# Three low parts a layer on GpSimd, two fewer tap pairs on TensorE, and another order in the first mixer and the cross heads

## The chip, the cores and the metric

One core of a Trainium2 chip runs the whole program: two decoder blocks on a sequence of 256 rows. The metric is the device time of one execution in microseconds. TensorE (PE), VectorE (DVE), ScalarE (ACT), GpSimd (POOL) and SyncE (SP) have instruction streams of their own, are written one by one in the kernel, and meet only at semaphores.

## What is computed

The reference is two networks one after the other. The first has two layers (a mixer, cross attention to a memory, a feed-forward with squared ReLU), the second two more. Cut to what matters here:

```python
# first block, layer 0: window attention and a gated linear recurrence, then memory_xattn, then the MLP
q, k, v, xr, gate = split(rms_norm(x) @ w_in)
o_a = dilated_window_attn(q, k, v)              # four heads ("at0")
xc = conv4(xr); a, u = gates(xc)
hs = associative_scan(a, u)                     # the scan
x = x + concat([o_a, hs * gelu(gate)]) @ w_out
x = x + memory_xattn(rms_norm(x), mem)          # four heads of 256 ("xa0", "xa1")
x = x + square(relu(rms_norm(x) @ w1)) @ w2

# second block, two layers
x = x + 0.5 * swiglu(rms_norm(x))
u = rms_norm(x) @ w_in
y = a * sigmoid(gate)                           # 384 channels
y = depthwise_conv(y, w_dw, taps=31) + b_dw     # causal, one filter a channel
y = silu(layer_norm(y))
o = sliding_window_attention(q, k, v, sinks)    # six heads ("sw", pairs 0 to 2), block 128
m = memory_attention(mq, mk, mv)                # four heads (pairs 3 and 4)
x = x + concat([y, o, m]) @ w_out
x = x + 0.5 * swiglu(rms_norm(x)); x = rms_norm(x)
```

## The kernel before

**Weights in units.** All weights pass as 269 units of 128 x 2048 (1 MB), in the order of use. For each unit SyncE issues a transfer into `raw`, ScalarE rounds it into `w_hi` (`highs`, L1024), and VectorE forms the low part, the rest `raw - w_hi`, in place of `raw` (`lows`, L1582). TensorE multiplies by high and low parts, so that two passes give nearly the precision of f32 (L360 to L362, L369 to L372, L405 to L407). There are 6 places for `raw` and the low parts and 4 for the high parts: a transfer waits until the unit six before it is used up, a high half until the unit four before. `highs(n)` and `lows(n)` work off all units up to n, and from unit 20 on one more (`prepared`). Unit numbers of a layer of the second block count from `u0`; `L_WO` = 42 is the first of the four units of its output projection, so `L_WO + 1` to `+ 3` are 43, 44 and 45.

**The order of the work** is written out by hand for each engine. An instruction that waits holds up all behind it on its engine. `mark` gives an instruction a semaphore count and `at` is what another waits for.

**First mixer.** TensorE sums the squares of the rows (`stream_sums`), VectorE turns the sums into a mean (`mean`, L1614), GpSimd takes the root (L2258), VectorE builds a diagonal matrix of it (`diagonal`, L1631), and TensorE spreads it over the columns (`spread`, L485). Between them VectorE also forms the low halves of the memory (`memory_low`, L1653). Later come the four heads: scores (L509), largest value and exponentials, `normalized` rows on VectorE (L1727, L1731), `turned` on TensorE (L519), copied by ScalarE, `product` (L529). The scan (L1914) and its gate (L1918) lie between them on VectorE. `key_columns` (L490) turns the normalized keys of the cross attention; tile t goes to its own PSUM bank, and bank 0 holds a value product before, which ScalarE copies out (`vxcopy`).

**Cross heads** (`cross`). For each of four heads TensorE makes the query, ScalarE squares it (L1317), VectorE adds and scales it (`query`, L1939, L1941), `soft` handles the maximum and ScalarE the exponentials, VectorE normalizes, TensorE turns and multiplies.

**Window stage of the second block.** The depthwise convolution has 384 channels, three blocks of 128. The third block is done on TensorE alone (`third_channel`, L895: products of 128 x 128 with diagonal-like tiles, 16 shifts times 2 groups, two taps each). Of the first two blocks VectorE does the first 24 taps (`run_taps`, one instruction of 128 x 256 a tap and block, L2109) and TensorE the last 7, as 4 shifts x 2 groups x 2 blocks. `third_channel(n)` issues the next n of these products, first those of the two shared blocks into bank 4; ScalarE copies their sums out (`second`, L1517) before the third block may use the bank. In between run the five pairs of heads: `window_scores` (L846, L852), VectorE's row maxima (`soft`: TENSOR_REDUCE L2147 and, for the window heads, a minimum with the sinks, L2153), ScalarE's exponentials (L1475), `window_turned` (L861), ScalarE's `turned_copy` (L1483), `window_product` (L874), `normalized_rows` (L2176), `rows_turned` (L921). GpSimd takes the roots of the head norms before this stage (L2258) and that of the channel variance (`cms`) behind it.

```python
def soft(i):
    nm = b.by_head(W_NM, range(2 * i, 2 * i + 2))                                  # in stat, SBUF
    for t in range(NT):
        m = dve.tensor_reduce(nm[:, t, :], W.scores(b, i, t), AX.X, ALU.max, negate=True)   # from PSUM
    if i < 3:
        sink = b.stat[:, W_NSINK + 2 * i:W_NSINK + 2 * i + 2].unsqueeze(1).broadcast_to([P, NT, 2])
        m = dve.tensor_tensor(nm, nm, sink, ALU.min)                               # both in SBUF
```

## Time and profile before

| | us |
|---|---|
| median of 3 runs (1679.78 to 1681.53) | 1679.93 |
| the profiled execution | 1680.01 |
| its span, first to last instruction | 1678.7 |
| TensorE matmuls busy | 1661.4 (99%) |
| VectorE busy | 1194.3 (71%) |
| ScalarE busy | 881.9 (53%) |
| GpSimd busy | 175.3 (10%) |

Busy shares say which engine is close to its limit, not how much a shorter instruction gives: matmuls overlap, so their busy time also covers gaps of up to 0.2 us. What an edit is worth is read from the starts of TensorE's instructions and from what it waits for. One matmul of f32 operands stands as two records in the trace.

### The profile page before, as it was taken

How to read it: one execution, taken by the hardware profiler on the slowest of the kernel's cores; microseconds unless marked ns; L12 is line 12 of the kernel's file. 1: busy time of each engine (PE TensorE's matmuls, PEld its weight loads, DVE VectorE, ACT ScalarE, POOL GpSimd, SP SyncE). 2: the span in 40 equal slices, each digit the busy share in tenths (PEclk: the TensorE clock that was granted, in tenths of full speed). 3: DMA queues.
4: the chain of work that ended last, by engine and by line, in shares of the span. 5: the costliest groups of instructions: out<-in, count | busy, mean ns of one | idle time of the engine just before them, and what ended most of it. 6: DMA issues, size and time to landing. Idle time of an engine off the chain costs nothing.

```text
span 1678.7 us, 24718 instructions
## 1 busy us (share of the span) xinstructions
PE 1661.4 (99%) x10347; PEld 1480.4 (88%) x10348; DVE 1194.3 (71%) x1450; ACT 881.9 (53%) x1094; POOL 175.3 (10%) x166
## 2 busy tenths in 40 slices
PE   8999999999999999999999999999999999999998
PEld 7889988888999888888889998888888899998887
DVE  7876477665656777577767877778687677787763
ACT  6655455444545455455544564556555545565552
POOL 0401010011101001200021110003200022010002
PEclk9999999999999999999999999999999999999999
DMA  8444345555434565555555335555554654145541
GB/s 338 170 150 158 115 167 195 183 194 204 161 112 163 189 214 188 193 191 178 202 222 197 117 110 191 179 197 203 184 195 182 236 203 176 51 176 188 188 181 46
DMA packets 42991, 297.39 MB, mean 177 GB/s; under 512 B 4864, under 2 KB 5632, under 8 KB 8448
## 3 DMA queue, kind: packets, MB, share of 16 engines
q1 hardware_dynamic: 39600, 282.61, 46.7%
q10 hardware_dynamic: 3280, 13.21, 2.1%
q8 instruction: 81, 1.33, 0.3%
q14 instruction: 30, 0.25, 0.1%
HBM read 294.75 MB, written 1.05 MB: 176 GB/s over the span
## 4 chain that ended last, share of the span: by engine, by line
PE 93%; DVE 4%; ACT 2%; DMA 1%; issue 1%; SPq 0%; POOL 0%; ACTq 0%; DVEq 0%
PE ps L372 38%; PE ps L371 19%; PE ps L360 4%; PE ps L362 4%; PE ps L361 4%; PE ps L369 4%; PE ps L405 3%; PE ps L407 3%; PE ps L406 3%; PE ps L370 2%; DVE w_lo L1582 1%; ACT w_hi L1024 1%; PE ps L895 1%; PE ps L529 1%; PE ps L874 1%
## 5 line engine op out<-in xcount | busy, mean ns | idle before, releaser
L1582 DVE TENSOR_TENSOR w_lo<-raw,w_hi 128x2048 fp32r<-128x2048 f32 x267 | 610.4, 2289 | 210.4 <-ACT w_hi L1024 206.6
L1024 ACT ACTIVATE w_hi<-raw 128x2048 fp32r<-128x2048 f32 x267 | 508.3, 1905 | 184.6 <-PE ps L372 117.8
L372 PE MATMUL ps<-xT,w_hi 128*128 128x512 f32 x1680 | 598.6, 396 | 0.0
L371 PE MATMUL ps<-xT,w_lo 128*128 128x256 f32 x1680 | 468.7, 279 | 0.0
L372 PE MATMUL ps<-hT,w_hi 128*128 128x512 f32 x1147 | 405.2, 397 | 0.0
L372 PEld LDWEIGHTS ps<-xT,w_hi 128*128 128x128 f32 x1680 | 315.3, 188 | 65.0
L371 PEld LDWEIGHTS ps<-xT,w_lo 128*128 128x128 f32 x1680 | 316.7, 189 | 11.2 <-DVE xT L1589 0.2
L371 PE MATMUL ps<-hT,w_lo 128*128 128x256 f32 x1147 | 321.4, 280 | 1.4 <-DVE hT L1781 1.4
L372 PEld LDWEIGHTS ps<-hT,w_hi 128*128 128x128 f32 x1147 | 215.4, 188 | 50.1
L371 PEld LDWEIGHTS ps<-hT,w_lo 128*128 128x128 f32 x1147 | 216.3, 189 | 4.7 <-DVE hT L1781 2.7
L1076 ACT ACTIVATE tmp<-ps 128x512 f32<-128x512 f32 x120 | 72.0, 600 | 254.5 <-PE ps L372 254.5
L2291 POOL TENSOR_TENSOR ff<-ff 128x256 f32<-128x256 f32 x70 | 94.1, 1344 | 962.7 <-ACT ff L1054 669.1
L360 PE MATMUL ps<-xT,w_hi 128*128 128x256 f32 x608 | 176.5, 290 | 1.8 <-DVE w_lo L1816 1.8
L362 PE MATMUL ps<-xT,w_hi 128*128 128x256 f32 x608 | 171.9, 283 | 0.0
L361 PE MATMUL ps<-xT,w_lo 128*128 128x256 f32 x608 | 171.9, 283 | 0.0
L1640 DVE TENSOR_TENSOR tmp<-ps,tmp 128x512 f32<-128x512 f32 x120 | 82.7, 689 | 83.6 <-ACT tmp L1076 83.4
L360 PEld LDWEIGHTS ps<-xT,w_hi 128*128 128x128 f32 x608 | 116.5, 192 | 3.2 <-DVE w_lo L1816 2.5
L361 PEld LDWEIGHTS ps<-xT,w_lo 128*128 128x128 f32 x608 | 116.5, 192 | 0.5
L362 PEld LDWEIGHTS ps<-xT,w_hi 128*128 128x128 f32 x608 | 116.4, 192 | 0.0
L369 PE MATMUL ps<-xT,w_hi 128*128 128x512 f32 x240 | 96.4, 403 | 0.0
L405 PE MATMUL ps<-w_hi,memT 128*128 128x256 f32 (+1 forms) x256 | 81.0, 317 | 0.0
L2258 POOL TENSOR_TENSOR stat<-stat,mhalf 128x2 f32<-128x2 f32 (+2 forms) x45 | 42.1, 944 | 365.1 <-DVE stat L1678 112.7
(282 smaller groups left out, 2003.6 us busy)
## 6 DMA issues: line engine op xcount, KB each, us to landing
raw<-weights_dram SPq DMA_DIRECT2D x263, 1024.0 KB, 4.8
tmp<-third_taps_dram ACTq DMA_DIRECT2D x2, 2048.0 KB, 9.2
raw<-weights_dram SPq DMA_DIRECT2D x4, 768.0 KB, 5.1
raw<-weights_dram SPq DMA_DIRECT2D x4, 512.0 KB, 8.5
tmp<-mem_dram ACTq DMA_DIRECT2D x2, 1024.0 KB, 7.0
x<-x_in_dram SPq DMA_DIRECT2D x2, 512.0 KB, 5.6
arena<-mem_dram ACTq DMA_DIRECT2D x1, 1024.0 KB, 10.4
arena<-pool_mat_dram ACTq DMA_DIRECT2D x1, 1024.0 KB, 6.9
```

Of the source, the lines that this page charges most:

```text
L360: pe.matmul(out, b.hi(u, cs), src[:, k, 0, :], start=first, stop=False)
L361: pe.matmul(out, b.lo(u, cs), src[:, k, 0, :], start=False, stop=False)
L362: return pe.matmul(out, b.hi(u, cs), src[:, k, 1, :], start=False, stop=last)
L369: pe.matmul(ps[:, bank, :].rearrange("p (a n) -> p a n", a=2), hi, src[:, k, :, :], start=True, stop=False)
L371: pe.matmul(ps[:, bank, 0:S], lo, src[:, k, 0, :], start=False, stop=False)
L372: return pe.matmul(ps[:, bank, :].rearrange("p (a n) -> p a n", a=2), hi, src[:, k, :, :], start=False, stop=last)
L405: pe.matmul(out, h, b.hi(u, cs), start=(first and j == 0), stop=False)
L1024: act.activation(b.hi(u, slice(0, width(u))), b.raw(u, slice(0, width(u))), ACT.Copy).then_inc(*mark("hi", u))
L1076: act.activation(tmp, ps[:, bank:bank + 2, S:2 * S], ACT.Copy).then_inc(*mark("half", name, j))
L1582: dve.tensor_tensor(b.lo(u, cs), b.raw(u, cs), b.hi(u, cs).bitcast(F32), ALU.subtract).then_inc(*mark("lo", u))
L1640: dve.tensor_tensor(dst, ps[:, bank:bank + 2, 0:S], tmp, ALU.add).then_inc(*mark(label, *((name, j) if label != "u32" else (name[:-1], j))))
L2291: pool.tensor_tensor(b.acc(), b.sq(0) if c == 1 else b.acc(), b.sq(c), ALU.add).then_inc(*mark("sqsum", f, c))
```

## The change

Four things change. The low parts of units 43, 44 and 45 of each layer of the second block are formed by GpSimd, after its roots of the head norms, and no longer by VectorE; TensorE waits for them by a semaphore of their own (`low_of`). `SHARED` goes from 4 to 2: VectorE does the first 28 taps of the first two blocks, TensorE the last 3, and the table of their tiles (`shared_taps`) is half as wide and lies in one place. The numbers of taps and products between the steps of the window stage are set anew, on ScalarE the memory values are copied before the first turned rows and the memory keys after the second sums. In the first mixer and the cross heads instructions stand in another order.

```diff
+GPSIMD_UNITS = frozenset(U_LAYER + PER_LAYER * l + L_WO + i for l in range(2) for i in (1, 2, 3))
+def low_of(u):
+    return ("lo_gpsimd" if u in GPSIMD_UNITS else "lo"), u
-SHIFTS, SHARED = 16, 4
+SHIFTS, SHARED = 16, 2
...
@@ TensorE, first mixer @@
-    pe.wait_ge(*at("vxcopy", 0, 2))
-    key_columns(0, 0, (0, 1))
+    key_columns(0, 0, (0, 1), (1, 0), lambda: pe.wait_ge(*at("vxcopy", 0, 2)))
...
@@ TensorE, window stage @@
         window_turned(0)
-        third_channel(4)
         window_turned(1)
...
         window_scores(2)
-        third_channel(4)
+        third_channel(6)
         window_product(1)
...
         memory_columns("mq", qr[:, :, 512:768])
-        third_channel(6)
+        third_channel(5)
...
@@ ScalarE, window stage @@
         soft(0)
         soft(1)
-        turned_copy(0)
...
         c.then_inc(*mark("mvcopy", l))
+        turned_copy(0)
         turned_copy(1)
-        memory_keys()
         act.wait_ge(*at("second_sum", l))
...
         i.then_inc(*mark("second", l))
+        memory_keys()
...
@@ ScalarE, behind the first feed-forward of a layer @@
-        for dst, cs in ((b.arena[:, 5, :], slice(0, 1024)), (b.arena[:, 15, 512:1024], slice(1024, 1536))):
-            act.dma_start(dst, d["shared_taps"][l, :, cs]).then_inc(*landed("d_shared", l, cs.start))
-        act.dma_start(b.slot2(0)[:, :, 768:1024],
-                      d["shared_taps"][l, :, 1536:2048].rearrange("p (a n) -> p a n", a=2)).then_inc(*landed("d_shared", l))
+        act.dma_start(b.arena[:, 5, :], d["shared_taps"][l]).then_inc(*landed("d_shared", l))
...
@@ VectorE, lows() @@
+            if u in GPSIMD_UNITS:
+                continue
...
@@ VectorE, first mixer @@
+    mean("x0", 4)
+    diagonal("x0")
     for c in range(4):
         memory_low("mem1", raw1, c)
-    mean("x0", 4)
     lows(4)
-    diagonal("x0")
...
     lows(16)
+    lows(17)
+    normalized("at0", 3, True)
+    head_low("at0", 1, slice(4, 6), 2)
     dve.wait_ge(*at("scan_in"))
...
-    lows(17)
-    head_low("at0", 1, slice(4, 6), 2)
-    normalized("at0", 3, True)
...
@@ VectorE, cross heads @@
         lows(uq + 4)
+        normalized(tag, 0)
         query(2)
-        normalized(tag, 0)
         soft(1)
+        normalized(tag, 1)
         lows(uq + 5)
         query(3)
-        normalized(tag, 1)
...
@@ VectorE, window stage @@
-        lows(u0 + L_MQ + 4)
-        run_taps(12)
+        run_taps(15)
         soft(2)
         run_taps(9)
         soft(3)
         sink_arguments()
-        lows(u0 + L_MK + 3)
-        run_taps(5)
+        run_taps(7)
         soft(4)
         normalized_rows(SWA)
+        run_taps(5)
+        row_lows(SWA)
         run_taps(4)
-        lows(u0 + L_MV + 3)
-        run_taps(3)
-        row_lows(SWA)
-        run_taps(2)
         normalized_rows(MEM)
...
@@ GpSimd, after the roots of the head norms @@
+        first = U_LAYER + PER_LAYER * l + L_WO + 1
+        for u in range(first, first + 3):
+            cs = slice(0, width(u))
+            pool.wait_ge(*at("hi", u))
+            pool.tensor_tensor(b.lo(u, cs), b.raw(u, cs), b.hi(u, cs).bitcast(F32),
+                               ALU.subtract).then_inc(*mark("lo_gpsimd", u))
```

Line numbers in what follows of the change are those of the changed file, which are up to 7 higher (L1582 is L1587 there, L2109 is L2114).

VectorE at the start of the window stage, before: row maxima of the first two pairs (L2147, L2153), a low part, taps (L2109).

```order
L1684 TENSOR_TENSOR arena<-ps,stat 128x256 x2
L2147 TENSOR_REDUCE stat<-ps 128x2 x2
L2153 TENSOR_TENSOR stat<-stat 128x2x2
L2147 TENSOR_REDUCE stat<-ps 128x2 x2
L2153 TENSOR_TENSOR stat<-stat 128x2x2
L1582 TENSOR_TENSOR w_lo<-raw,w_hi 128x2048
L2109 SCALAR_TENSOR_TENSOR arena<-arena,par 128x256 x12
L2147 TENSOR_REDUCE stat<-ps 128x2 x2
L2153 TENSOR_TENSOR stat<-stat 128x2x2
L2109 SCALAR_TENSOR_TENSOR arena<-arena,par 128x256 x9
```

And of the change:

```order
L1689 TENSOR_TENSOR arena<-ps,stat 128x256 x2
L2152 TENSOR_REDUCE stat<-ps 128x2 x2
L2158 TENSOR_TENSOR stat<-stat 128x2x2
L2152 TENSOR_REDUCE stat<-ps 128x2 x2
L2158 TENSOR_TENSOR stat<-stat 128x2x2
L2114 SCALAR_TENSOR_TENSOR arena<-arena,par 128x256 x15
L2152 TENSOR_REDUCE stat<-ps 128x2 x2
L2158 TENSOR_TENSOR stat<-stat 128x2x2
L2114 SCALAR_TENSOR_TENSOR arena<-arena,par 128x256 x9
```

The low part between the second minimum and the first taps is gone, and 15 taps follow instead of 12.

GpSimd at the same place, of the change: the roots of the head norms, then the three low parts, then the root of the channel variance and the sums of squares. Before, the row of L2380 is not there.

```order
L2371 MEMSET arena 128x8
L2259 TENSOR_TENSOR stat<-stat,mhalf 128x8 x2
L2259 TENSOR_TENSOR stat<-stat,mhalf 128x4 x4
L2380 TENSOR_TENSOR w_lo<-raw,w_hi 128x2048 x3
L2259 TENSOR_TENSOR stat<-stat,mhalf 128x2
L2292 TENSOR_TENSOR ff<-ff 128x256 x6
```

They stand behind the four roots of four columns (two each for the memory queries and keys of the window stage), and nothing but their high halves holds them.

VectorE in the first mixer before, from the normalized rows of the third head (L1731): low part, scan (L1914), gate (L1918), low part, low half of the first heads (L1737), then the last head's rows (L1720 to L1731).

```order
L1731 TENSOR_SCALAR arena<-arena,stat 128x256
L1582 TENSOR_TENSOR w_lo<-raw,w_hi 128x2048
L1914 SCALAR_TENSOR_TENSOR arena<-arena 128x256 x4
L1918 SCALAR_TENSOR_TENSOR arena<-arena 128x1024
L1582 TENSOR_TENSOR w_lo<-raw,w_hi 128x2048
L1737 TENSOR_TENSOR xT<-ps,xT 128x2x256
L1720 SCALAR_TENSOR_TENSOR arena,stat<-arena,tmp 128x128
L1720 SCALAR_TENSOR_TENSOR arena,stat<-arena,tmp 128x256
L1727 RECIPROCAL stat<-stat 128x2
L1731 TENSOR_SCALAR arena<-arena,stat 128x128
L1731 TENSOR_SCALAR arena<-arena,stat 128x256
```

And of the change:

```order
L1736 TENSOR_SCALAR arena<-arena,stat 128x256
L1587 TENSOR_TENSOR w_lo<-raw,w_hi 128x2048 x2
L1725 SCALAR_TENSOR_TENSOR arena,stat<-arena,tmp 128x128
L1725 SCALAR_TENSOR_TENSOR arena,stat<-arena,tmp 128x256
L1732 RECIPROCAL stat<-stat 128x2
L1736 TENSOR_SCALAR arena<-arena,stat 128x128
L1736 TENSOR_SCALAR arena<-arena,stat 128x256
L1742 TENSOR_TENSOR xT<-ps,xT 128x2x256
L1922 SCALAR_TENSOR_TENSOR arena<-arena 128x256 x4
L1926 SCALAR_TENSOR_TENSOR arena<-arena 128x1024
```

Both low parts and the last head's rows now stand before the scan.

## Rows read from the trace of the kernel before

**Rows 1.** The page, parts 1 and 2: TensorE's busy time, and its granted clock.

```profile
PE 1661.4 (99%) x10347; PEld 1480.4 (88%) x10348; DVE 1194.3 (71%) x1450; ACT 881.9 (53%) x1094; POOL 175.3 (10%) x166
PEclk9999999999999999999999999999999999999999
```

**Rows 2.** TensorE's waits: us in total, times, longest.

```profile
PE ps L519 <- DVE arena L1731: 3.3, 5, 1.4
PE ps L485 <- DVE ff L1631: 2.4, 2, 1.9
...
PE ps L490 <- ACT tmp L1137: 0.3, 1, 0.3
```

**Rows 3.** Timeline near the first spread: start, us, engine, line, operation, [idle].

```profile
25.68 0.16 DVE L1614 TENSOR_SCALAR stat<-ps 128x2 f32<-128x2 f32 x1
27.08 2.29 DVE L1582 TENSOR_TENSOR w_lo<-raw,w_hi 128x2048 fp32r<-128x2048 f32 x1 [1.18 <-ACT w_hi L1024]
...
29.83 0.70 PE L485 MATMUL ps<-ff,cst 128*128 128x256 f32 x2 [1.89 <-DVE ff L1631]
```

**Rows 4.** Timeline of TensorE: product and transposes, without and with a wait.

```profile
107.48 0.81 PE L529 MATMUL ps<-arena 128*128 128x256 f32 x4
108.13 0.49 PE L519 MATMUL ps<-cst,arena 128*128 128x128 f32 x3
...
113.95 0.81 PE L529 MATMUL ps<-arena 128*128 128x256 f32 x4
116.13 0.55 PE L519 MATMUL ps<-cst,arena 128*128 128x128 f32 x3 [1.37 <-DVE arena L1731]
```

**Rows 5.** Timeline of TensorE: the first of four such waits in the cross heads.

```profile
171.35 0.66 PE L519 MATMUL ps<-cst,arena 128*128 128x128 f32 x4 [0.48 <-DVE arena L1731]
```

**Rows 6.** Timeline of TensorE: eight calls of the grouped products.

```profile
944.04 1.95 PE L895 MATMUL ps<-pairs,arena 128*128 128x128 f32 x16
945.83 0.60 PE L911 MATMUL ps<-cst,arena 128*128 128x128 f32 x4
```

**Rows 7.** GpSimd beside VectorE: one line's min/median/max in ns, then timelines.

```profile
L2291 POOL TENSOR_TENSOR ff<-ff x70: 733/891/2542, 146.3 to 1663.1; 128x256 f32<-128x256 f32 x70
...
48.92 2.54 POOL L2323 TENSOR_TENSOR arena<-arena 128x1024 f32<-128x1024 f32 x1
49.23 2.50 DVE L1853 SCALAR_TENSOR_TENSOR arena<-arena,sm 128x256 f32<-128x256 f32 x1
...
74.83 2.41 POOL L2339 TENSOR_TENSOR arena<-arena 128x1024 f32<-128x1024 f32 x1 [6.62 <-ACT arena L1243]
...
1178.12 3.02 POOL L2304 TENSOR_TENSOR ff<-ff 128x256 f32<-128x256 f32 x2 [7.89 <-ACT ff L1048]
1180.60 0.41 DVE L1795 TENSOR_TENSOR ff<-ps,ff 128x256 f32<-128x256 f32 x1
```

**Rows 8.** Timelines of the window stage of the first layer, by engine.

```profile
939.40 1.98 POOL L2258 TENSOR_TENSOR stat<-stat,mhalf 128x4 f32<-128x4 f32 x2 [1.13 <-DVE stat L1678]
...
944.08 0.16 DVE L2153 TENSOR_TENSOR stat<-stat 128x4 f32<-128x4 f32 x1
...
946.36 4.83 DVE L2109 SCALAR_TENSOR_TENSOR arena<-arena,par 128x256 f32<-128x256 f32 x12
...
936.55 1.96 ACT L1024 ACTIVATE w_hi<-raw 128x2048 fp32r<-128x2048 f32 x1
...
943.08 2.60 ACT L1475 ACTIVATE arena<-ps,stat 128x128 f32<-128x128 f32 x8 [3.26 <-DVE stat L2153]
947.12 0.81 ACT L1483 ACTIVATE arena<-ps 128x768 f32<-128x768 f32 x1 [1.44 <-PE ps L861]
947.83 0.83 ACT L1508 ACTIVATE arena<-ps,stat 128x256 f32<-128x256 f32 x2
...
947.82 0.82 PE L861 MATMUL ps<-cst,arena 128*128 128x128 f32 x6
948.76 0.41 PE L874 MATMUL ps<-arena 128*128 128x65 f32 x2
```

More of the change, by code:

```diff
@@ L177, in taps_of @@
         j = 2 * SHARED * block + 2 * (s - SHIFTS + SHARED) + g
-        place, at = ((5, P * j) if j < 8 else (15, 512 + P * (j - 8)) if j < 12 else ((j - 12) // 2, 768 + P * (j % 2)))
-        return self.arena[:, place, at:at + P]
+        return self.arena[:, 5, P * j:P * j + P]
     def by_head(self, col, heads):
@@ L374, in up_unit @@
     def up_unit(u, bank, of=None):
-        pe.wait_ge(*at("lo", u))
+        pe.wait_ge(*at(*low_of(u)))
         if of is None:
@@ L388, in head_unit @@
     def head_unit(u, bank, of=None):
-        pe.wait_ge(*at("lo", u))
+        pe.wait_ge(*at(*low_of(u)))
         out = b.pair(bank)
@@ L415, in rows_units @@
                 between(k)
-            pe.wait_ge(*at("lo", u))
+            pe.wait_ge(*at(*low_of(u)))
             for t in range(NT):
@@ L424, in value_unit @@
     def value_unit(u, bank):
-        pe.wait_ge(*at("lo", u))
+        pe.wait_ge(*at(*low_of(u)))
         for t in range(NT):
@@ L435, in out_projection @@
             u = u0 + i
-            pe.wait_ge(*at("lo", u))
+            pe.wait_ge(*at(*low_of(u)))
             if i < 3:
@@ L491, in chunk_transposes, with key_columns @@
         return last
-    def key_columns(l, pair, banks):
+    def key_columns(l, pair, banks, order=(0, 1), between=None):
         tag = f"xk{l}{pair}"
-        for t in range(NT):
+        for t in order:
             pe.wait_ge(*at("hrow", tag, t))
+            if between and t == order[1]:
+                between()
             chunk_transposes(banks[t], b.k_rows(pair)[:, t, :], 4).then_inc(*mark("ctr", tag, t))
@@ L563, in feed_forward @@
                 if at_tile % 16 == 0:
-                    pe.wait_ge(*at("lo", v))
+                    pe.wait_ge(*at(*low_of(v)))
                 if oc == 0 and kc % 2 == 0:
@@ L659, in tensor_program @@
     u = U_KEYS[0][1]
-    pe.wait_ge(*at("lo", u))
+    pe.wait_ge(*at(*low_of(u)))
     for t in range(NT):
@@ L665, in tensor_program @@
     turned("at0", 2, 0)
-    pe.wait_ge(*at("lo", u + 1))
+    pe.wait_ge(*at(*low_of(u + 1)))
     for t in range(NT):
@@ L681, in second_keys @@
         if (k, bk) == (5, 0):
-            pe.wait_ge(*at("kcol", "xk00", 1))
+            pe.wait_ge(*at("kcol", "xk00", 0))
             key_columns(0, 1, (0, 1))
@@ L752, in tensor_program @@
     feed_forward("mlp0", U_FF[0], False, sums_in_6("mlp0"), spread_in_6("mlp0"))
-    pe.wait_ge(*at("lo", U_POOL))
+    pe.wait_ge(*at(*low_of(U_POOL)))
     for g in range(4):
@@ L828, in memory_tile @@
                 last.then_inc(*mark("unit", u))
-        pe.wait_ge(*at("lo", u0 + L_MK))
+        pe.wait_ge(*at(*low_of(u0 + L_MK)))
         pe.wait_ge(*at("hrow", f"qk{l}", 0))
@@ L836, in tensor_program @@
             chunk_transposes(1 + t, qr[:, t, 0:512], 4).then_inc(*mark("ctr", f"qk{l}", t))
-        pe.wait_ge(*at("lo", u0 + L_MV))
+        pe.wait_ge(*at(*low_of(u0 + L_MV)))
         pe.wait_ge(*at("hrow", f"qk{l}", 1))
@@ L940, in tensor_program @@
         window_turned(2)
-        third_channel(6)
+        third_channel(5)
         window_product(2)
@@ L945, in tensor_program @@
         window_turned(3)
-        third_channel(5)
+        third_channel(4)
         rows_turned(SWA)
@@ L1125, in head_high, with key_copies @@
                        ACT.Copy).then_inc(*mark("ohi", tag, i))
-    def key_copies(tag, dst8, banks, pair):
-        for t in range(NT):
+    def key_copies(tag, dst8, banks, pair, order=(0, 1)):
+        for t in order:
             act.wait_ge(*at("ctr", tag, t))
@@ L1300, in scalar_program @@
     head_high("at0", 3, slice(6, 8), 3, U_V + 1)
-    key_copies("xk00", b.k8(), (0, 1), 0)
+    key_copies("xk00", b.k8(), (0, 1), 0, (1, 0))
     key_copies("xk01", b.k8(), (0, 1), 1)
```

## The prediction

> **What bounds the kernel now.** I read the page's busy times first: TensorE is busy 99% of the span, at its upper clock of 2.4 GHz in every slice [rows 1]. Busy matmuls overlap, so I then read TensorE's waits: all that the profile names are some 12 us, and three of them lie where this change works [rows 2]. So TensorE's own stream of instructions sets the time. An edit is worth what it takes out of that stream, or out of a stall in it, and work moved between the other engines costs nothing until something that TensorE waits for comes late. The places themselves are read in the timeline, from start to start. The profiled execution took 1680.0 us, of which its span is 1678.7 and 1.3 lie around it; the median of the three runs is 1679.9, so I work from 1680.0.
>
> **First mixer, the spread of x0.** TensorE waits 1.89 for VectorE's diagonal [rows 3]. VectorE reads the column sums at 25.68, behind four memory lows, and then works on a low part from 27.08 to 29.3 before it builds the diagonal [rows 3]. In the new order the mean and the diagonal stand before both. The low part ahead of them ends near 23.2; with 0.3 for the two small operations, 0.7 for GpSimd's root and 0.5 for the diagonal it is there at about 25, before TensorE is at the spread (27.9). The low part behind it begins at 27.08 because it waits for its high half [rows 3], so it isn't late. The wait is gone.
>
> **The heads.** TensorE waits 3.3 us in five places for normalized softmax rows: once 1.37 in the first mixer [rows 4], four times 0.48 in the two cross attentions (one is shown [rows 5]), and 0.28 for a value copy before the first key columns [rows 2]. In the mixer the rows stand behind scan, gate and a low part on VectorE; in the new order VectorE, which ends the low part before that at 108.3, does one more until 110.5 and has the rows at 112.0, before TensorE starts the third product at 113.95. The scan's result comes 4.4 later (a low part, the softmax rows, a head's low half), near 116.3; the low half made from it is wanted by the second unit of the output projection, near 129. In the cross heads the exponentials are done some 4 us before the query for which VectorE now no longer waits first. The key columns in the order 1, 0 put 0.43 of transposes ahead of the wait for the copy. All six waits go: 1.9 + 3.3 + 0.3 = 5.5. With each wait a restart goes too: 113.95 to 116.13 is 2.18, the same pair without a wait 0.65 (107.48 to 108.13) [rows 4], so 1.53 are lost where the wait is 1.37. I take 0.16 for each of six: 1.0. **Gain 6.5.**
>
> **The convolution.** The grouped products were 48 calls a layer (16 of the first two blocks, 32 of the third) and are 40. A call is two records; 16 records take from 944.04 to 945.83 [rows 6], so a call is 0.224 and 8 are **1.8 a layer**, all in TensorE's stream. VectorE gets 8 more taps of 0.40 (12 in 4.83 [rows 8]), 3.2, and gives away three low parts of 2.3: by its own time it is better off by 3.7. The shared taps come in one transfer instead of three, long before they are read: nothing.
>
> **The low parts on GpSimd.** This decides. An addition of 256 columns takes GpSimd 0.73 at best, one of 1024 columns 2.41 [rows 7]: 2.19 ns a column, so 4.65 for 2048. And it does not run beside VectorE: a VectorE step on two SBUF operands, which takes 0.40 a piece in a row of them [rows 8], took 2.50 when it began 0.3 behind a GpSimd operation of 2.54, that is, it ended with it [rows 7]. An operation with one operand in PSUM passes: 0.41 at 1180.60, while GpSimd is at work until 1181.14 [rows 7]. The Trainium skill, GPSIMD Engine Reference, section Performance versus the Vector engine, has 4.5 us for an addition of 2048 columns; by it each low part would hold VectorE 0.15 less and the sum below would be 0.9 lower.
>
> So I lay out the window stage anew, in the first layer (the second has the same rows 482 us later). GpSimd is free at 941.4 (939.40 + 1.98) and the high halves of units 43 and 44 are written (the second at 938.5) [rows 8]: low parts from 941.4 to 946.0 and on to 950.7. VectorE's row maxima read PSUM and pass, but each pair ends in a minimum of 4 columns on two SBUF operands. The first minimum, due at 942.9, gets in at 946.0 between the two low parts; the second, 944.08 before [rows 8], is held until 950.7. ScalarE's exponentials of that pair (1.3, half of 2.60 [rows 8]) end at 952.1, and TensorE, which turned the pair at 947.82, does so at 952.2. Behind the exponentials ScalarE has a value copy of 0.83 and a copy of turned rows of 0.81, so the first product starts at 953.9 instead of 948.76 [rows 8]: **5.1 late**. Of the 8 calls that are gone, 4 lay before it and are swallowed; 4 lie behind it and give 0.9 back.
>
> VectorE from there: 15 taps end at 956.8, the third maximum 958.0, 9 taps 961.6, the fourth 962.9, 7 taps 965.8, the fifth, whose scores are late too, 967.5, the rows of the window heads 968.9, where TensorE asks at 968.7. Then the third low part, whose high half is written behind the fourth pair's exponentials, starts at 967.5 and holds the next 5 taps until 972.1; the rows of the memory heads come at 977.7, where TensorE asks at 976.8. These two waits are 1.1, of which I count 0.5, since waits of 0.1 to 0.3 that the stretch has anyway (the first product waited 0.29 behind the transposes: 0.94 instead of 0.65 [rows 8]) vanish in them. **Loss 5.1 - 0.9 + 0.5 = 4.7 a layer**; the 1.8 saved is inside it. Queued behind the low parts on GpSimd is only the root of the channel variance, wanted 12 us after the last of them, and TensorE reads units 43 to 45 later still.
>
> **Sum:** 1680.0 - 6.5 + 2 x 4.65 = **1682.8**. What a measurement can tell from no change is 0.2%, 3.4 us: 1676.6 to 1683.3.
>
> **Bounds of what the trace doesn't show.** Whether an operation of 4 columns is held: from below nothing, from above the rest of the low part. I take the upper end, since the rows that are held and those that pass differ by their operands. The Trainium skill, SBUF — State Buffer, section Who interferes with whom, has the rule without a width in it: two SBUF inputs are enough to be locked out for the whole GpSimd instruction. By the rule the sum is 1682.8; if only wide operations are held it is rival (a). Whether 2048 columns hold as 1024 do: from below nothing (c), from above longer (b).
>
> **Rivals.**
> (a) Only the taps are held. Then the first product starts at 948.0, but the taps begin at 950.7 instead of 946.36, of which 15 end near 956.4; third maximum, exponentials and transposes follow late, and TensorE's line turns into waits one after the other. I get 3.3 a layer: 1680.0 - 6.5 + 6.7 = **1680.2**. For it: nothing so narrow was seen held.
> (b) The other side: a low part is longer beside VectorE than its width says. The median of 256 columns is 0.89 against 0.73 [rows 7]; by that ratio, 1.22, a low part is 5.7. Two stand before the second minimum and the third before the memory rows, so each us on a low part is 3 a layer: 1682.8 + 6 x 1.0 = **1689**. It decides from 4.75 on. Against it: the 1024 columns at 48.92, with VectorE held, took 2.54, only 0.13 more than alone. TensorE also stands still for 4 us here; the granted clock never leaves its upper level in this trace [rows 1], and the longest gap in TensorE's starts is 2.2 [rows 4]. The Trainium skill, TensorE: Matmul & The Clock Gate, Part 1, lets an idle TensorE fall to half its clock; no row here shows it, and it would add to this case.
> (c) No hold at this width. Then each layer saves its 1.8 and the small waits before the first product, 2.3: 1680.0 - 6.5 - 4.6 = **1668.9**. Against it: the 2.50.
> (d) The hold is real, but the stage has more slack than I find, and its loss and the 1.8 cancel: **1673.5**, the first block's gain alone.
>
> **How the numbers follow.** Forecast 0.34, (a) 0.22, (b) 0.18, (c) 0.14, (d) 0.12. The forecast lies 0.5 under the edge of what counts as slower: 0.22 within, 0.12 slower; (a) 0.18 within, 0.03 faster, 0.01 slower. Faster 0.29, within 0.40, slower 0.31. The range reaches to (c) below, which the rows don't exclude, and nearly to (b) above: 1668 to 1688. The forecast's own is 1680 to 1685.
>
> **What would show it.** In the first 500 us the waits of 1.9, 1.4, 0.3 and four of 0.5 gone from TensorE's list. GpSimd's low parts at 4.6 us. In the window stage a minimum of 3 to 4 us instead of 0.16, a tap of 4, and a TensorE wait of about 4 for ScalarE's exponentials of the second pair. I am wrong if the minimum stays at 0.16 and the first product isn't late, if the taps aren't held, or if the first block's waits come back at another tile.

## The result, and the profile after

| | before | changed |
|---|---|---|
| median of 6 runs each, us | 1680.0 | 1686.8 |
| lowest to highest | 1679.8 to 1681.8 | 1685.4 to 1689.0 |
| the profiled execution, and its span | 1680.0, 1678.7 | 1686.9, 1685.5 |

The ratio is 1.0039, 95% interval 1.0027 to 1.0051: slower by 0.4%. The forecast was 1682.8, with a range of 1668 to 1688, of which 1680 to 1685 was the forecast's own and the rest was there for its rivals. Each ratio further down is to runs of the kernel before that were taken beside it, with medians of 1679.9 to 1680.6; one run of e2, 2731.9 us at a mean clock of 0.555, is left out as slow.

The page of the changed kernel, in the lines of [rows 1]; each digit of the second is the granted clock in tenths, in a fortieth of the span. (All lines of code stand 5 to 7 further down: L868 was L861, L902 was L895, L2158 was L2153.)

```profile
PE 1664.7 (99%) x10316; PEld 1485.0 (88%) x10316; DVE 1205.0 (71%) x1460; ACT 881.3 (52%) x1094; POOL 202.3 (12%) x172
PEclk9999999999999999999999899999999999899999
```

The clock line now has two digits of 8. They are the slices in which the two window stages lie. TensorE's waits, with the total, the number of times and the longest, as in [rows 2]:

```profile
PE ps L868 <- ACT arena L1478: 9.1, 4, 3.6
...
PE ps L491 <- DVE ff L1636: 0.5, 1, 0.5
...
PE ps L928 <- DVE arena L2181: 0.3, 2, 0.2
```

Of [rows 2], the 3.3 for the softmax rows and the 0.3 for the value copy are gone, and of the two waits for a diagonal only the one of 0.5 at the end of the program is left. In their place stands one group: the transposes of the window stage (L868) wait 9.1 for ScalarE's exponentials, in each layer once 0.96 for the first pair and once 3.59 for the second. Next the window stage of the first layer, by engine. POOL's two rows are the low parts, DVE's are the row maxima (L2152), the minima (L2158) and taps (L2114), and the last four are TensorE's:

```profile
934.48 9.04 POOL L2380 TENSOR_TENSOR w_lo<-raw,w_hi 128x2048 fp32r<-128x2048 f32 x2
964.09 4.54 POOL L2380 TENSOR_TENSOR w_lo<-raw,w_hi 128x2048 fp32r<-128x2048 f32 x1 [20.58 <-ACT w_hi L1030]
...
936.00 3.07 DVE L2158 TENSOR_TENSOR stat<-stat 128x4 f32<-128x4 f32 x1
939.00 1.01 DVE L2152 TENSOR_REDUCE stat<-ps 128x2 f32<-128x256 f32 x2
940.11 3.43 DVE L2158 TENSOR_TENSOR stat<-stat 128x4 f32<-128x4 f32 x1
943.46 6.01 DVE L2114 SCALAR_TENSOR_TENSOR arena<-arena,par 128x256 f32<-128x256 f32 x15
...
965.98 4.51 DVE L2114 SCALAR_TENSOR_TENSOR arena<-arena,par 128x256 f32<-128x256 f32 x5
...
937.17 1.95 PE L902 MATMUL ps<-pairs,arena 128*128 128x128 f32 x16
...
944.98 1.54 PE L868 MATMUL ps<-cst,arena 128*128 128x128 f32 x6 [3.59 <-ACT arena L1478]
946.50 2.79 PE L881 MATMUL ps<-arena 128*128 128x65 f32 x12
...
977.35 1.46 PE L963 MATMUL ps<-arena,cst 128*128 128x256 f32 x6
```

Two low parts take 9.04, so 4.52 each. The minimum of 4 columns, 0.16 before [rows 8], takes 3.07 and 3.43. Each ends with a low part: 936.00 + 3.07 = 939.07 and 934.48 + 4.52 = 939.00, then 943.54 and 943.52. The second minimum is what ScalarE's exponentials wait for, and TensorE stands still for 3.59. The reductions between them, which read PSUM, take 1.01 for two as ever. The third low part holds taps: five of them take 4.51 from 965.98, where five took 2.06 before.

The third view is the same stage cut into stretches, with the granted clock behind the busy times:

```profile
934.00:945.00 11.00, 6.45 (x55) 5.78 (x51) 10.25 (x11) 2.78 (x9) 9.52 (x3) 0.96 0.27 95
945.00:955.00 10.00, 10.00 (x50) 8.63 (x51) 7.81 (x21) 4.48 (x10) 0.00 (x0) 0.54 0.00 0
955.00:965.00 10.00, 10.00 (x85) 9.06 (x85) 7.14 (x18) 6.25 (x13) 0.91 (x1) 1.00 0.01 2
```

Behind the wait the clock is 0.54 for 10 us: nearly all of that time at the lower of its two levels, 1.2 GHz. TensorE is busy 10.00 of 10.00 there, but does 50 matmul records, where the next stretch does 85.

A measure for all that follows is the **length of the stage**: from the first grouped product (L902, 937.17 above; 944.04 before, [rows 6]) to the products that sum the channels of the convolution (L963, 977.35 above; 977.09 before). It is read in the profiled execution, which took 1685.7 in e6 and 1683.3 in e9, and elsewhere is within 0.6 of the median. Outside the stage and the first block the kernels take the same time, within 0.5.

| kernel | stage starts | length, 1st layer | 2nd layer | median us |
|---|---|---|---|---|
| before | 944.04 | 33.05 | 33.05 | 1680.0 |
| changed | 937.17 | 40.18 | 39.55 | 1686.8 |
| e1 low parts on VectorE | 937.17 | 33.21 | 36.42 | 1676.6 |
| e2 order of the first block alone | 937.32 | 33.06 | 33.03 | 1672.9 |
| e3 minimum by scalar | 936.86 | 38.45 | 41.85 | 1687.1 |
| e4 transposes 5 times | 937.20 | 36.56 | 39.75 | 1683.4 |
| e5 low parts behind the minima | 937.17 | 38.12 | 39.65 | 1684.4 |
| e6 16 products in the wait | 936.88 | 40.75 | 38.10 | 1683.3 |
| e7 sinks in PSUM | 937.01 | 34.80 | 34.81 | 1677.1 |
| e8 low parts behind the taps | 937.02 | 31.25 | 31.24 | 1669.9 |
| e9 8 products in the wait | 937.05 | 36.54 | 39.73 | 1681.8 |
| e10 e7 and two small operations | 936.80 | 35.06 | 35.05 | 1676.9, one run |
| e11 as e8, one tap pair less | 936.69 | 31.01 | 31.00 | 1668.6 |
| e12 transposes 7 times | 936.90 | 36.57 | 36.57 | 1680.1 |

The changed kernel is 6.9 earlier at the stage and loses 7.13 and 6.50 in it: -6.87 + 13.63 = 6.8, the whole of its 6.8.

### The profile page after: what moved, and what is told of

The parts are those of the page before. It is cut to its first block, busy times and chain, and to the rows that moved or that the text cites. A ratio compares the mean times of both kernels' runs of the same rounds, so it can differ in the third digit from the quotient of the medians.

```text
span 1685.5 us, 24667 instructions
## 1 busy us (share of the span) xinstructions
PE 1664.7 (99%) x10316; PEld 1485.0 (88%) x10316; DVE 1205.0 (71%) x1460; ACT 881.3 (52%) x1094; POOL 202.3 (12%) x172
## 4 chain that ended last, share of the span: by engine, by line
PE 93%; DVE 4%; POOL 1%; ACT 1%; issue 1%; DMA 0%; SPq 0%; DVEq 0%
PE ps L378 38%; PE ps L377 19%; PE ps L366 5%; PE ps L367 4%; PE ps L368 4%; PE ps L375 4%; PE ps L411 3%; PE ps L413 3%; PE ps L412 3%; PE ps L376 2%; PE ps L881 1%; POOL stat L2259 1%; PE ps L517 1%; PE ps L537 1%; PE ps L902 1%; DVE w_lo L1587 1%
## 5 line engine op out<-in xcount | busy, mean ns | idle before, releaser
L1587 DVE TENSOR_TENSOR w_lo<-raw,w_hi 128x2048 fp32r<-128x2048 f32 x261 | 596.6, 2289 | 204.2 <-ACT w_hi L1030 200.0
L411 PE MATMUL ps<-w_hi,memT 128*128 128x256 f32 (+1 forms) x256 | 81.1, 317 | 0.0
L413 PE MATMUL ps<-w_hi,memT 128*128 128x256 f32 (+1 forms) x256 | 79.4, 310 | 0.0
```

Of the source, the lines that this page charges most:

```text
L411: pe.matmul(out, h, b.hi(u, cs), start=(first and j == 0), stop=False)
L413: last = pe.matmul(out, l, b.hi(u, cs), start=False, stop=(last_k and j == len(ks) - 1))
L1587: dve.tensor_tensor(b.lo(u, cs), b.raw(u, cs), b.hi(u, cs).bitcast(F32), ALU.subtract).then_inc(*mark("lo", u))
```

## The experiments

### e2: the order of the first block alone

The kernel before, with the edits in the first mixer and the cross heads and nothing else.

```diff
...
     lows(3)
+    mean("x0", 4)
+    diagonal("x0")
     for c in range(4):
         memory_low("mem1", raw1, c)
-    mean("x0", 4)
     lows(4)
-    diagonal("x0")
...
     lows(16)
+    lows(17)
+    normalized("at0", 3, True)
+    head_low("at0", 1, slice(4, 6), 2)
...
         lows(uq + 4)
+        normalized(tag, 0)
         query(2)
-        normalized(tag, 0)
...
```

> The kernel before with the new order of the first mixer and the cross heads alone. The theory: this part of the change is worth the 6.9 us by which TensorE stands earlier at the window stage in the changed kernel: 1673.1, between 1672.5 and 1674. Rival (a part of those 6.9 is given back later, since weights come no earlier, or belongs to other edits): 1675 to 1680, and TensorE waits after the first block that neither trace has.

Measured: 1672.9, ratio 0.9954 (0.9941 to 0.9967). The stage starts at 937.32, 6.7 earlier than before, and takes 33.06 and 33.03, as before. So this part is worth what its seven waits and the restarts behind them were, nothing of it is given back, and the loss of the changed kernel is all in the rest of the change.

### e1: low parts back on VectorE

The changed kernel with `lows` at the places of before, and without the three on GpSimd.

```diff
-GPSIMD_UNITS = frozenset(U_LAYER + PER_LAYER * l + L_WO + i for l in range(2) for i in (1, 2, 3))
+GPSIMD_UNITS = frozenset()
...
+        lows(u0 + L_MQ + 4)
         run_taps(15)
         soft(2)
         run_taps(9)
         soft(3)
         sink_arguments()
+        lows(u0 + L_MK + 3)
         run_taps(7)
         soft(4)
         normalized_rows(SWA)
         run_taps(5)
+        lows(u0 + L_MV + 3)
...
```

> The changed kernel, but VectorE forms all low parts again, at the places of before. The theory (the low parts on GpSimd hold VectorE's second minimum, TensorE stands still for 3.6 us and then runs at its lower clock): only the gains are left, 6.9 in the first block as the traces show and 1.8 a layer for the 8 calls less: 1680.0 - 6.9 - 3.6 = 1669.5; up to 1672 if VectorE, which has 3.2 us of taps more a layer than before, comes late with the memory heads' rows. The minimum is back at 0.16, no TensorE wait over 1 us in the window stage, granted clock 1.00 there. Rival (the loss comes from the new numbers of taps and products between the steps, not from GpSimd): 1680 or more, with a wait of several us left in the window stage.

Measured: 1676.6, ratio 0.9975 (0.9965 to 0.9985). The 3.6 us wait is gone, but the time is 4.6 above the upper end that I gave. The timeline of TensorE at the turning of the window heads' rows, first and second layer, and then the stretches behind the wait in each:

```profile
959.15 0.87 PE L928 MATMUL ps<-cst,arena 128*128 128x128 f32 x6 [2.13 <-DVE arena L2181]
...
1441.61 0.88 PE L928 MATMUL ps<-cst,arena 128*128 128x128 f32 x6 [2.11 <-DVE arena L2181]
```

```profile
962.00:970.00 8.00, 8.00 (x71) 8.00 (x70) 7.22 (x15) 3.12 (x6) 0.00 (x0) 1.00 0.01 2
...
1443.00:1450.00 7.00, 7.00 (x37) 7.00 (x37) 5.25 (x9) 1.68 (x4) 0.00 (x0) 0.54 0.00 0
```

Two things that I had not seen. VectorE's own line is full: with 8 taps more it has the rows 2.1 late, which eats the 1.8 of the 8 calls (33.21 against 33.05; e8 tests this). And behind a wait of 2.1 the clock came down in the second layer, though not in the first: 36.42 - 33.21 = 3.2 us.

### e3, e7, e10: which operations GpSimd holds

e3 forms the minimum with the sink as a scalar for each partition, so that one tensor is read from SBUF. e7 keeps the instruction and puts the sinks of the first two pairs into PSUM. e10 is e7 with two operations more behind the second minimum, on one tensor in SBUF with a constant.

```diff
@@ e3 @@
-                m = dve.tensor_tensor(nm, nm, sink, ALU.min)
+                for side in range(2):
+                    at0 = W_NSINK + 2 * i + side
+                    m = dve.tensor_scalar(nm[:, :, side], nm[:, :, side], b.stat[:, at0:at0 + 1], None, ALU.min)
@@ e7 @@
+        sinks_ps = ps[:, 7, 400:404]
+        dve.tensor_scalar(sinks_ps, b.lp("sinks")[:, 0:4], -1.0, None, ALU.mult).then_inc(*mark("sink_ps", l))
...
+                sink = sinks_ps[:, 2 * i:2 * i + 2] if i < 2 else b.stat[:, W_NSINK + 4:W_NSINK + 6]
@@ e10, behind soft(1) @@
+        dve.tensor_scalar(nsink, nsink, 1e30, None, ALU.min)
+        dve.tensor_scalar(wide, wide, 1e30, None, ALU.min)
```

> The changed kernel, but the minimum of the row maxima with the sinks is two operations with the sink as a scalar for each partition, so each reads one tensor in SBUF instead of two; the low parts stay on GpSimd and start as before. If it is the two SBUF operands that are held: the minima take under 0.3 us each while GpSimd is at work, the 3.6 us wait and the fall of the clock are gone, and the taps alone are held: about 1680 (1678 to 1683). If every operation on SBUF is held by GpSimd: the first of the two takes 3 us as now, and the time stays at 1686.8 (1686 to 1688).

> The changed kernel, but the minima of the first two pairs read the negated sinks from PSUM (written there by a small operation before the stage) instead of from SBUF: the same tensor_tensor of 128x4, with one operand in each memory. If only an operation with both inputs in SBUF is held: 0.16 to 0.3 each while GpSimd works, the 3.6 us wait is gone, and the taps alone are held, which is my rival (a) by itself: about 1677 (1673.5 to 1681). If an operation that reads or writes SBUF at all is held: 3 us each as now, and 1686.8 (1685 to 1688.5).

> The kernel with the sinks in PSUM (e7), with two small operations more on VectorE behind the second minimum, while GpSimd is at work on the two low parts: a tensor_scalar with a constant on 4 columns of SBUF, in place, and the same on 64 columns (constants so large that nothing changes). They read one operand in SBUF and no scalar from there. If only a second read of SBUF is held: 0.1 to 0.2 each, near 937.2, and the taps behind them are held as in e7. If every operation that reads and writes SBUF is held: the first takes 1.5 us or more.

Measured: e3 1687.1, ratio 1.0038 (1.0025 to 1.0050). e7 1677.1, ratio 0.9986 (0.9977 to 0.9995). e10, one run, 1676.9. The timelines of e3, of e7 and of e10, GpSimd's row first in each:

```profile
934.16 9.03 POOL L2381 TENSOR_TENSOR w_lo<-raw,w_hi 128x2048 fp32r<-128x2048 f32 x2
935.68 7.53 DVE L2159 TENSOR_SCALAR stat<-stat 128x2 f32<-128x2 f32 x2
```

```profile
934.38 9.25 POOL L2384 TENSOR_TENSOR w_lo<-raw,w_hi 128x2048 fp32r<-128x2048 f32 x2
935.89 0.16 DVE L2162 TENSOR_TENSOR stat<-stat,ps 128x4 f32<-128x4 f32 x1
...
937.07 0.16 DVE L2162 TENSOR_TENSOR stat<-stat,ps 128x4 f32<-128x4 f32 x1
937.15 11.92 DVE L2114 SCALAR_TENSOR_TENSOR arena<-arena,par 128x256 f32<-128x256 f32 x15
```

```profile
934.17 9.11 POOL L2388 TENSOR_TENSOR w_lo<-raw,w_hi 128x2048 fp32r<-128x2048 f32 x2
936.86 0.16 DVE L2162 TENSOR_TENSOR stat<-stat,ps 128x4 f32<-128x4 f32 x1
936.93 1.85 DVE L2167 TENSOR_SCALAR stat<-stat 128x4 f32<-128x4 f32 x1
938.70 0.18 DVE L2169 TENSOR_SCALAR trig<-trig 128x64 f32<-128x64 f32 x1
```

In e7 the same instruction on the same 4 columns takes 0.16 in the middle of a low part, because one of its operands is in PSUM; in the changed kernel it took 3.07. This settles rival (a): 4 columns are held as wide ones are, and the place of the operands decides. The rest of e7 is (a)'s case by itself, the taps alone held: 15 of them take 11.92 instead of 6.01, and the stage takes 34.80 in both layers.

The first of my two cases for e3 fell, and with it my words for the rule: "two operands in SBUF" is too narrow. A tensor_scalar with one tensor in SBUF is held too, 7.53 for two, so e3 gains nothing: TensorE's wait grows to 5.4, and the median is that of the changed kernel within the spread of the runs (1683.8 to 1691.0). A scalar from SBUF is not what does it: in e10 the operation has a constant, and takes 1.85, until 938.78, where the first low part ends (934.17 and half of 9.11: 938.73). By the Trainium skill, SBUF — State Buffer, section Who interferes with whom, `tensor_scalar` can use both of VectorE's ports for its one tensor and then meets GpSimd; the trace agrees with the 1.85. In all rows shown here what passed in the middle of a GpSimd instruction had an operand in PSUM.

### e5: the low parts behind the second minimum

```diff
         for u in range(first, first + 3):
             cs = slice(0, width(u))
+            pool.wait_ge(*at("mx", f"sw{l}", 1))
             pool.wait_ge(*at("hi", u))
```

> The changed kernel, but GpSimd's low parts wait for the second minimum (near 937.3). Theory now: VectorE's own line is as tight as TensorE's here (with all low parts on VectorE, TensorE still waited 2.1 us for the rows of the window heads), so a hold costs wherever it lies. The minima take 0.16, the 3.6 us wait is gone, but the first taps end near 946.4 + 6, some 7 us later than in the kernel with the low parts on VectorE; TensorE waits about 5 us for the exponentials of the third pair and its clock falls there instead: 1683 (1680 to 1687). Rival (only the hold of the minimum costs, the taps have slack): 1673 to 1676.

Measured: 1684.4, ratio 1.0022 (1.0013 to 1.0031). The minima take 0.16, but the timeline has this for the taps and for TensorE's next transposes, and behind them the stretch with the clock reads 0.71:

```profile
937.27 14.57 DVE L2114 SCALAR_TENSOR_TENSOR arena<-arena,par 128x256 f32<-128x256 f32 x15
...
954.49 1.54 PE L868 MATMUL ps<-cst,arena 128*128 128x128 f32 x6 [4.27 <-ACT arena L1478]
```

```profile
955.00:963.00 8.00, 8.00 (x51) 7.55 (x50) 7.27 (x20) 4.28 (x7) 1.55 (x1) 0.71 0.00 0
```

The hold has moved from the minima to the taps, 14.57 - 6.01 = 8.6 us of it, and comes out as a wait of 4.27 one pair later, with the clock down behind it. A low part on GpSimd held VectorE for some 4.3 us here (8.6 for two) where VectorE makes it in 2.3, so it is only cheap where VectorE reads PSUM or is idle.

### e4, e12: what the clock costs

Both leave everything late that is late, and give TensorE something to do in the wait: the first pair's transposes again, 4 times in e4 and 6 times in e12.

```diff
-            for side in range(2):
+            for side in [0, 1] * times:
...
-        window_turned(0)
+        window_turned(0, 5)
```

> The changed kernel, but TensorE repeats the transposes of the first pair four times (2.6 us of work that changes nothing) ahead of its wait of 3.6 us, so the wait is there and TensorE isn't idle in it for more than 1 us. If the idle time is what lets the clock fall: the granted clock stays at 1.00 behind it, the first product starts at the same time and what follows takes 2.5 to 3 us less a layer: 1681.3 (1680.5 to 1682.5). Rival (the clock falls for another reason, or its fall costs nothing because later waits swallow it): 1686.8, between 1685.5 and 1688.

> As the kernel that repeats the first pair's transposes four times in the wait (e4), but six times, which fills the 1.0 us that was left of it; nothing else changes, and the product behind it starts at the same time. In e4 the clock stayed up in the first layer, where the stage ended 3.6 earlier than in the changed kernel, and fell in the second, where it ended no earlier. If the idle time is the cause and the clock costs 3.5 a layer: it now stays up in both, 1679.9 (1679 to 1681). If the clock falls for another reason in the second layer: 1683.4 as e4.

Measured: e4 1683.4, ratio 1.0013 (1.0005 to 1.0022), 0.9 above my range. e12 (with 7 for the 5) 1680.1, ratio 0.9998 (0.9989 to 1.0007). The stretches of e12, as above for the changed kernel, and TensorE's product and its twelve records of third-block products at either clock, of e12 and of the changed kernel:

```profile
945.00:955.00 10.00, 9.45 (x83) 8.24 (x82) 9.43 (x24) 6.18 (x16) 0.00 (x0) 1.00 0.01 2
```

```profile
946.25 1.52 PE L881 MATMUL ps<-arena 128*128 128x65 f32 x12 [0.55 <-ACT arena L1486]
...
948.89 1.60 PE L902 MATMUL ps<-pairs,tmp 128*128 128x128 f32 x12
950.33 0.89 PE L881 MATMUL ps<-arena 128*128 128x65 f32 x7
```

```profile
951.44 2.93 PE L902 MATMUL ps<-pairs,tmp 128*128 128x128 f32 x12
954.16 0.39 PE L881 MATMUL ps<-arena 128*128 128x65 f32 x2
```

The first product starts at 946.25, 9.35 behind the start of the stage, where the changed kernel has 946.50 and 9.33, so the hold is all still there. But the clock stays at 1.00: twelve records take 950.33 - 948.89 = 1.44, where they take 954.16 - 951.44 = 2.72 in the changed kernel. The stage takes 36.57 in both layers instead of 40.18 and 39.55, 6.6 us in all, and the median falls by 6.7. The changed kernel and e12 differ in these transposes alone, so that is the price of the clock, apart from the hold. In e4 TensorE still stood idle for 1.00 and, six transposes later, for 0.65; the clock stayed up in the first layer (36.56) and fell in the second (39.75).

### e6, e9: useful work in the wait

The third block's products are TensorE's own spare work. e6 puts 16 of them ahead of the wait, e9 8; both move the copy of the second sums, which they need, ahead of the second pair's exponentials on ScalarE.

```diff
         window_turned(0)
+        third_channel(16)
         window_turned(1)
...
         soft(0)
+        act.wait_ge(*at("second_sum", l))
...
+        i.then_inc(*mark("second", l))
         soft(1)
```

> The changed kernel, but 16 of the third block's products stand ahead of TensorE's wait of 3.6 us, with the copy of the second sums on ScalarE moved ahead of the exponentials of the second pair so that they may start. The same work in all. The theory (the idle time is lost, and the clock falls because of it): 3.6 of work move into the wait, less 0.7 for the copy, and the clock stays up, which gives 2.5 to 3 more, less what VectorE's rows then make TensorE wait: 1676 (1674.5 to 1679.5). Rival (the clock's fall costs nothing): 1681. Rival (VectorE's later rows are the bound, so that time gained here is waited for there): 1684 to 1687.

> As the kernel with 16 products in the wait (e6), but 8, so that the other 8 stay as cover for the waits later in the stage. My reading of e6 (its profile): the wait was filled and the clock stayed up there, but from 955 on TensorE had no products left and waited 0.45, 1.76 and 1.11 for copies and rows, and the clock fell at 964 instead. If that is right: 1.8 of the wait filled, no wait over 1.3 left in the stage, the clock stays up in at least one layer: 1678 (1676.5 to 1681.5). If it is wrong (the order in which ScalarE now copies costs it): 1683 as e6, or more.

Measured: e6 1683.3, ratio 1.0025 (1.0012 to 1.0038), with runs from 1679.8 to 1692.1; e9 1681.8, ratio 1.0009 (1.0000 to 1.0018). e6 missed my number by 7 and the upper end of my range by 3.8. TensorE in e6, from the place where its products are used up, and the clock before and behind it:

```profile
956.79 1.55 PE L881 MATMUL ps<-arena 128*128 128x65 f32 x12 [0.45 <-ACT arena L1487]
...
962.19 0.87 PE L928 MATMUL ps<-cst,arena 128*128 128x128 f32 x6 [1.76 <-DVE arena L2182]
...
968.24 1.97 PE L881 MATMUL ps<-arena 128*128 128x65 f32 x8 [1.11 <-ACT arena L1487]
```

```profile
945.00:955.00 10.00, 9.99 (x87) 8.79 (x87) 9.43 (x24) 4.71 (x12) 0.00 (x0) 1.00 0.01 2
...
964.00:972.00 8.00, 6.88 (x33) 6.49 (x32) 5.12 (x12) 2.40 (x5) 0.69 (x1) 0.50 0.01 2
```

The products filled the wait and kept the clock up there, but they had been cover for later waits, which now lie open, and the clock falls at 964 instead (in the second layer near 1459). e9 leaves 8 for later: its stage takes 36.54 in the first layer, 3.6 less than the changed kernel, and 39.73 in the second, where the clock falls again. Its runs go from 1680.3 to 1683.4, and the median is 0.3 above my range. Work that only moves TensorE's idle time didn't win it back here, since VectorE's rows come when they come.

### e8, e11: both gains without the hold

e8 is e1 with two of the three low parts put where VectorE is idle, behind the taps. e11 takes one more tap pair from TensorE (`SHARED` 1, 4 products a layer fewer, 4 taps more).

```diff
@@ e8, against e1 @@
-        lows(u0 + L_MK + 3)
         run_taps(7)
...
-        lows(u0 + L_MV + 3)
         row_lows(SWA)
...
         row_lows(MEM)
+        lows(u0 + L_MK + 3)
         dve.wait_ge(*at("chsum", l))
...
+        lows(u0 + L_MV + 3)
@@ e11 @@
-SHIFTS, SHARED = 16, 2
+SHIFTS, SHARED = 16, 1
```

> The kernel with all low parts on VectorE (e1), but those of units 44 and 45 stand behind the taps and behind the centring, where VectorE is idle for 2.5 and 3.9 us, instead of between the taps. TensorE wants them near 977 and 984. Theory: the wait of 2.1 us for the rows of the window heads in e1 comes from VectorE's line; without it both gains are there in full: 1680.0 - 6.9 - 3.6 = 1669.5 (1668.5 to 1671), granted clock 1.00 in both window stages. Rival (the products saved give nothing, because the stage is bound by the chain of maxima, exponentials and transposes): 1673 to 1675, with TensorE waits of over 1 us at other places of the stage.

> The best kernel so far (e8) with one tap pair more moved from TensorE to VectorE: 36 products a layer instead of 40, 4 taps more on VectorE, where it waited 1.76 us for the products of the memory heads. If 4 products are 0.9 us of TensorE's stream and the 4 taps (1.6) fit: 1669.9 - 1.8 = 1668.1 (1667.4 to 1669). If VectorE's line is now full: 1669.5 to 1672, with TensorE waits for the rows of the memory heads or for the conv sums.

Measured: e8 1669.9, ratio 0.9939 (0.9927 to 0.9951); e11 1668.6, ratio 0.9929 (0.9917 to 0.9942). VectorE's low parts and TensorE's turning of the window heads' rows in e8, then the same turning in e11:

```profile
937.12 2.28 DVE L1587 TENSOR_TENSOR w_lo<-raw,w_hi 128x2048 fp32r<-128x2048 f32 x1
...
967.20 2.28 DVE L1587 TENSOR_TENSOR w_lo<-raw,w_hi 128x2048 fp32r<-128x2048 f32 x1
970.64 2.28 DVE L1587 TENSOR_TENSOR w_lo<-raw,w_hi 128x2048 fp32r<-128x2048 f32 x1
...
957.03 0.87 PE L928 MATMUL ps<-cst,arena 128*128 128x128 f32 x6 [0.15 <-DVE arena L2181]
```

```profile
956.47 0.88 PE L928 MATMUL ps<-cst,arena 128*128 128x128 f32 x6 [0.76 <-DVE arena L2181]
```

In e8 the wait of 2.13 is 0.15, no wait of the stage is over 0.34, and the stage takes 31.25: 1.80 and 1.81 less than before; 8 calls of 0.224 are 1.79. e11 saves 4 calls more, 0.9, but its waits grow by 0.6 and the stage gets 0.24 shorter: VectorE's line is full again. The time falls in my first range (1667.4 to 1669) and the waits are those of my second; of the 1.4 between e8 and e11 only 0.5 lies in the two stages. These two beat both kernels, by 0.6% and 0.7% against the one before.

## Why the prediction was right about the hold and left out the clock

**First block: right.** I had 6.5; the traces give 6.9 in the changed kernel and 6.7 in e2, with all the waits gone and none at another tile. They are seven, though, not six (one for the diagonal, five for softmax rows, one for the value copy), so the term for restarts was 1.1 and my sum 6.6. The diagonal is there at 25.2, against my "about 25".

**Length of a low part: right.** 4.65 from the widths, 4.52 measured, so rival (b), 5.7, falls.

**Held or not: right, with the rule too narrow.** I took the upper end for the 4 columns, since rows held and rows passed differ by their operands. The minimum is held for 3.07 and 3.43, and e7 shows the operand as the cause. (a) falls, and so does (c). That one tensor in SBUF is enough, with a constant, I hadn't seen (e10); it changed nothing in the sum. "A tap of 4" among the signs was too long: the five taps beside the third low part lose 4.51 - 2.06 = 2.45 in all. e7 also gives the price of (a): 34.80 - 33.05 = 1.75 a layer, where I had 3.3. My chain of late maxima was too long: of the 5.9 by which the first taps end late, 1.6 reach TensorE at the next transposes and 1.8 at the rows.

**The wait of the first product: right.** I had its start 5.1 late; it is 946.50 - (948.76 - 6.87) = 4.6.

**The 8 calls: right as a price, wrong as a gain by themselves.** e8 has the 1.80. But I wrote that VectorE is better off by 3.7 and looked no further. With the low parts on VectorE (e1) its line is so full that 2.1 of wait take the place of the 1.8.

**The clock: here the sum failed.** The step is "Loss 5.1 - 0.9 + 0.5 = 4.7 a layer". e12, with the same hold and the clock up, gives 36.57 - 33.05 = 3.5 for it, 1.2 less than I had: the first product is 0.5 less late, and the later waits of 0.5 don't come (0.15 at L928), although the third low part holds its taps there too. The changed kernel itself gives 7.1 and 6.5. The difference, 3.6 and 3.0, is the lower clock, nearly half of the whole loss of 13.6. I named it in rival (b) as something that would add, and gave it no price and no place in the sum. By the Trainium skill, TensorE: Matmul & The Clock Gate, Part 1, an idle TensorE falls to half its clock, a rule that I weighed and set aside because no row of before showed it. Nor did any row of before show TensorE idle for 4 us; the lack of a row was no evidence. The trace agrees: 0.54 over 945 to 955 behind the wait of 3.59.

The two errors are of opposite sign: 1680.0 - 6.9 + 2 x 3.5 = 1680.1 is what the kernel takes at the upper clock (e12 has 1680.1), and 6.6 for the clock make it 1686.7. So the time came to lie 1.8 above what I gave as the forecast's own, and 3.5 past the edge of what counts as slower, to which I had given a chance of 0.31. It lies within 1668 to 1688 by luck: the upper end stood there for (b), a low part of 5.7, and that isn't what happened.

**(d), slack that cancels the loss: wrong.** With the clock up (e12) the stage is still 3.5 longer than before. There is some slack: of the 5.9 in e7 TensorE sees 1.63 + 1.79 = 3.4. But in e5, where the hold lies on the taps alone, it costs 5.1 and 6.6 a layer with the clock.

## What to carry to other kernels

An operation that looks free on an idle GpSimd was paid by VectorE here, for up to its whole length, in every kind of instruction tried that has all its tensors in SBUF, also at 4 columns; look for the one whose result the bottleneck waits for, and ask where VectorE is idle or reads PSUM. When a change makes TensorE stand still for longer than it did before, in one piece or in several close together, price the clock behind it as well: here it cost 6.6, and the two long waits were 7.2. And when work is taken from the bottleneck and given to an engine at 71%, lay out that engine's line through the stage first: the average said that there was room, and the gain came only when two low parts were moved out of the full stretch.

## What the runs showed of the hardware that I had not expected

- The fall of the clock isn't a function of the wait's length alone. With 2.13 and 2.11 of idle time at the same instruction (e1) it stayed up in the first layer and fell in the second; after 1.63 and 1.79 (e7) it stayed up in both layers of the trace, though three of the 11 runs of e7 took 3.2 more than that one (1679.7 to 1679.9, mean clock 0.997 to 0.998); after 1.00 and 0.65 close together (e4) it stayed up once and fell once. These falls cost 3.2 each (39.75 - 36.56, 36.42 - 33.21, 39.73 - 36.54). The spread of a kernel's runs goes with it: e6 goes from 1679.8 with a mean clock of 1.000 to 1692.1 with 0.992, and e12, with no wait over 1.0 in the stage, from 1679.9 to 1680.3. That the falls make the spread is argued, not shown: the kernel before goes from 1679.4 to 1682.6 (mean clock 1.000 to 0.998), with no wait over 1.9. What decides in a given run stays open.
- A fall seems to cost less the more of it lies in the wait; two layers suggest it, and no run was made for it. In the changed kernel the clock is down for about 10 us in both layers. In the first it falls near 944.0 (1.00 from 943 to 944, 0.51 from 944 to 945), 1.0 before the wait ends, and costs 3.6. In the second it falls some 2.2 before the end (an estimate from 0.86 over 1430 to 1433, with the wait ending at 1434.41) and costs 3.0.
- Repeated transposes kept the clock up: in e12 TensorE does nothing else from 940.24 to 945.7, and the clock is 1.00 throughout.
- Between two instructions of GpSimd that stand back to back VectorE gets in. In the changed kernel the first minimum ends with the first low part, and two reductions later the second is held by the second low part. In e10 an operation of 0.18 slips in at 938.70.
- Where the two meet, GpSimd hardly loses: the two low parts took 9.04 beside small operations, 9.25 in e7 and 9.38 in e5 beside the taps, which themselves lost 5.9 and 8.6.
